# Five of a turn's 25 key units summed over the head dimension by ScalarE, in a hybrid decoder step

## The chip, the cores and the metric

One Trainium2 chip; the kernel runs on one of its cores. The metric is the device time in microseconds (us) of one execution. TensorE (PE) does matrix products, VectorE (DVE) elementwise work and sums, ScalarE (ACT) activations and copies, GpSimd (POOL) here only starts transfers, SyncE (SP) starts transfers too. Each engine works through its own stream in order, and waits on semaphores for the others.

## The reference

The reference is one inference step of a two-layer hybrid decoder, for a prompt of 1024 tokens and for 8 sample sequences of one token each with 8192 past positions. The part around the change is the attention of the samples to their past keys, which lie in pages of 128 positions. Cut to it:

```python
def score(qb, kb):
    return jnp.einsum('bthd,bshd->bhts', qb, kb, preferred_element_type=jnp.float32) * scale + bias_h

def sb_weights(z, q_pos, k_pos):
    causal = k_pos[None, :] < q_pos[:, None]
    u = jnp.where(causal, jax.nn.log_sigmoid(-z), 0.0)
    after = lax.cumsum(u, axis=z.ndim - 1, reverse=True) - u
    return jnp.where(causal, jnp.exp(jax.nn.log_sigmoid(z) + after), 0.0)
```

With one query, a score is the sum over the 64 values of a head of query times key. There are 8 heads, 64 pages for each of the 8 samples, so 512 pages of 128 x 512 float32 (256 KB each), and as many pages of values. Beside it the same layer runs a recurrence (RWKV-7) over the prompt, in chunks of 64 tokens.

## The kernel before, in words

The kernel is a row of phases, each with a stream for every engine. The pages are a side job that is spread over several of them by the class `Pages`. A unit is two pages of keys; there are 256 units, 32 for each sample. For a unit `keys_dve` (L1097) waits for its two pages, multiplies them by the query on VectorE into `pg_prod` (L1106, 128x1024), and sums the 64 values of each head, also on VectorE, into `pg_z` (L1109). The units are dealt out by hand: 16 in `v_phase`, 42 in `pb_phase`, 24 in `attention_phase`, and from unit 82 on 25 in each turn of the recurrent stage, `rwkv_phase`.

Keys come over SyncE: `load_keys` (L1011) goes through the pages in order, waits until the slot of the ring (`RING` = 8 pages, so four units) is free, reads the page's number and starts the transfer. The slot counts as free when `k_used` says that the product of the unit four before is done. Values come over GpSimd (`load_values`, L1063) into a ring of 12 pages and are used by TensorE (`values_pe`, L1036).

When all units of a sample are done, `bias_dve` (L1118) adds the bias, `logs_act` (L1071) takes Abs, Exp and Ln on ScalarE, `softplus_dve` (L1126), `sums_pe` (L1031) and `exponents_dve` (L1131) make the exponents, and `weights_act` (L1079) the weights.

`rwkv_phase` runs turns `i` = 0 to 8. In a turn the local part of chunk pair `i` (products in a block, five levels of a triangular inverse), the walk of the state through pair `i-1` (two halves) and the preparation of pair `i+1` are interleaved in an order written out by hand for each engine. On VectorE the calls `more(n)` put the key units in between: with offsets in the turn, 0 to 2 after `softplus_dve`; 3, 4 after `blocks_t`; `state(i-1, 0)`, `blocks` and `exponents_dve`; 5; `mask_keys`, `gate_ones(i+1)`; 6, 7; `level(i, 1)`, `tanh(i+1)`, `keys(i+1)`; 8, 9; `lora_bias(i+1)`, `state(i-1, 1)`; 10; `level(i, 2)`, `sigmoid_ones(i+1)`; 11, 12; `log_decays(i+1)`, `center(i-1)`; 13, 14; `level(i, 3)`; 15, 16; `modified_keys(i+1)`, `normed(i-1)`, `level(i, 4)`; 17, 18; `products(i+1)`, `level(i, 5)`, `bonus(i+1)`, `outputs(i-1)`; 19 to 24; `bias_dve(i+1)`. Turn 7 has no units; the update of the samples' recurrent state takes their place. On ScalarE the order of a turn is `eyes`, `token_major`, `copy_read(i-1, 0)`, `copy_values(i-1, 0)`, `copy_blocks`, `copy_outputs(i-1, 0)`, `gate_exps(i+1)`, `copy_y(i, 1)`, `weights_act`, `copy_read(i-1, 1)`, `fold_act`, `copy_values(i-1, 1)`, `gate_sigmoids(i+1)`, `key_squares(i+1)`, `copy_y(i, 2)`, `sigmoid_exps(i+1)`, `copy_outputs(i-1, 1)`, `sigmoids(i+1)`, `copy_y(i, 3)`, `pick_act`, `key_norms(i+1)`, `decays(i+1)`, `output_squares(i-1)`, `copy_y(i, 4)`, `output_norms(i-1)`, `affine(i-1)`, `copy_y(i, 5)`, `logs_act(i+1)`.

Of the kernel before, what the change touches and what calls it, by code (L numbers as in the profile page):

```python
# [789 lines left out]
def v_phase(T):  # L790
# [8 lines left out]
    with ExitStack() as ctx:  # L799
# [47 lines left out]

        @block.vector
        def _(dve):
            pages.start_dve(dve)  # L850
            for k in range(KT):
                dve.wait_ge(w_rounded, k + 1)
                rest_weights(dve, wl[:, k, :], w[:, k, :], wh[:, k, :], w_split)
            pages.keys_dve(dve, KEYS_V)
# [101 lines left out]
class Pages:  # L956
# [8 lines left out]
    def __init__(self, T, ctx):  # L965
        nc = T.nc
        self.T, self.nc = T, nc
        self.sems = sems = Sems(nc, "pages")
        self.k_in = [sems(f"k_in{n}") for n in range(self.RING)]
        self.v_in = [sems(f"v_in{n}") for n in range(self.VRING)]  # L970
        (self.qc_in, self.q_turned, self.q_copied, self.q_stored, self.q_in, self.table_in, self.k_used, self.v_used,
         self.reduced, self.biased, self.logged, self.softplus_ready, self.summed, self.z_ready, self.w_ready,
         self.cleared, self.folded, self.selected, self.picked, self.step, self.act_step) = (
            sems(n) for n in ("qc_in", "q_turned", "q_copied", "q_stored", "q_in", "table_in", "k_used", "v_used",
                              "reduced", "biased", "logged", "softplus_ready", "summed", "z_ready", "w_ready",
                              "fold_cleared", "folded", "selected", "picked", "page_step", "page_act_step"))
        sb = lambda n, s, d=F32: ctx.enter_context(nc.sbuf_tensor("pg" + n, s, d))
        self.kp = sb("_k", [P, self.RING, D_A])
        self.qc, self.q = sb("_qc", [P, 4, NS]), sb("_q", [P, 2, D_A])
        self.fold = sb("_fold", [P, D_A])  # L980
        self.qr = self.fold[0:NS, :]
        self.prod = sb("_prod", [P, 2, D_A])
        self.z = sb("_z", [P, self.ZRING, H_A, NPG])
        self.zb, self.sp = sb("_zb", [P, H_A * NPG]), sb("_sp", [P, H_A * NPG])
        self.wts = sb("_w", [P, 2, H_A * NPG])
        self.table = sb("_table", [1, NS * NPG], I32)
        self.q_rows = nc.dram_tensor("scratch_pg_q", [NS, D_A], F32, kind="Internal").ap()
        self.fetched, self.unit = 0, 0
# [16 lines left out]

    def load_q(self, sp, b):
        if b >= 2:
            sp.wait_ge(self.k_used, self.RING + NPG * (b - 1))
        sp.dma_start(self.q[:, b % 2, :], self.q_rows[b:b + 1, :].to_broadcast([P, D_A])).then_inc(self.q_in, 16)

    def load_keys(self, sp, units):  # L1011

        for g in range(self.fetched, min(2 * units + self.RING, NS * NPG)):
            if g % NPG == NPG // 2 and 2 <= g // NPG + 1 < NS:
                self.load_q(sp, g // NPG + 1)
            n = g % self.RING
            sp.wait_ge(self.k_used, g + 1)
            page = sp.value_load(self.table[0:1, g:g + 1], min_val=0, max_val=self.T.n_phys - 1)
            sp.dma_start(self.kp[:, n, :], self.T.io["k_pages"][bass.ds(page, 1), :, :].rearrange("a p n -> (a p) n"))\
              .then_inc(self.k_in[n], 16)  # L1020
            self.fetched = g + 1
# [75 lines left out]
    def keys_dve(self, dve, n):  # L1097

        for u in range(self.unit, min(self.unit + n, NS * self.UNITS)):
            b, g, at = u // self.UNITS, 2 * u % NPG, 2 * u % self.RING  # L1100
            if g == 0:
                dve.wait_ge(self.q_in, 16 * b + 16)
            for e in range(2):
                dve.wait_ge(self.k_in[at + e], 16 * (2 * u // self.RING) + 16)
            dve.wait_ge(self.reduced, u + 1)
            dve.tensor_tensor(self.prod[:, :, :], self.kp[:, at:at + 2, :],  # L1106
                              self.q[:, b % 2, :].unsqueeze(1).to_broadcast([P, 2, D_A]), ALU.mult).then_inc(self.k_used, 2)
            dve.wait_ge(self.k_used, self.RING + 2 * u + 2)
            dve.tensor_reduce(self.z[:, b % self.ZRING, :, g:g + 2].rearrange("p h n -> p n h"),  # L1109
                              self.prod[:, :, :].rearrange("p n (h d) -> p n h d", h=H_A), AX.X, ALU.add)\  # L1110
               .then_inc(self.reduced, 1)
            self.unit = u + 1

    def start_dve(self, dve):
        dve.sem_inc(self.k_used, self.RING)
        dve.sem_inc(self.reduced, 1)

    def bias_dve(self, dve, b):  # L1118
        assert self.unit >= self.UNITS * (b + 1)
        dve.wait_ge(self.reduced, self.UNITS * (b + 1) + 1)  # L1120
# [18 lines left out]


KEYS_V, KEYS_PB, KEYS_ATT, KEYS_TURN = 16, 42, 24, 25


def attention_phase(T):
# [239 lines left out]
def rwkv_phase(T):  # L1384
# [23 lines left out]
    with ExitStack() as ctx:  # L1408
# [48 lines left out]
        @block.sync  # L1457
        def _(sp):
            pages.load_keys(sp, NS * Pages.UNITS)
            sp.wait_ge(pages.k_used, Pages.RING + NS * NPG)  # L1460
# [338 lines left out]
        def _(act):  # L1799
# [157 lines left out]
            for i in range(NPAIR + 1):  # L1957
# [7 lines left out]
                    sample_rows(0)  # L1965
                if walk:
                    copy_values(i - 1, 0)
                if local:
                    copy_blocks(i)
                if walk:  # L1970
                    copy_outputs(i - 1, 0)
                both(i, gate_exps)
                if local:
                    copy_y(i, 1)
                    pages.weights_act(act, i)
                else:
# [9 lines left out]
                    copy_values(i - 1, 1)  # L1986
                both(i, gate_sigmoids)
                both(i, key_squares)
                if local:
                    copy_y(i, 2)  # L1990
                else:
                    output_norms(SMP)
                both(i, sigmoid_exps) if walk else sigmoid_exps(1)
                if walk:
                    copy_outputs(i - 1, 1)
                both(i, sigmoids) if walk else sigmoids(1)
                if local:
                    copy_y(i, 3)
                else:
                    affine(SMP)  # L2000
                if walk:
# [3 lines left out]
                if walk:  # L2005
                    output_squares(i - 1)
                else:
                    sigmoid_exps(SMP)
                    sigmoids(SMP)
                if local:  # L2010
                    copy_y(i, 4)
                if walk:
# [9 lines left out]
                    sample_rows(2)  # L2022
                if i == 1:
                    sample_columns()
                if i + 1 < NS:
                    pages.logs_act(act, i + 1)

# [1172 lines left out]
```

## Time and profile before

| | before |
|---|---|
| median of 3 runs | 4680.5 us (4674.18 to 4684.39) |
| the profiled execution's own time | 4680.36 us |
| its span | 4678.8 us |
| busy: PE, DVE, ACT, POOL | 3892.4, 2356.6, 1174.4, 399.8 us |
| share of the span | 83%, 50%, 25%, 9% |
| DMA moved | 512.41 MB, mean 110 GB/s |

```profile
PE   6887885776777869999896999789898087999899
DVE  2488888888887224443312444444443524434411
ACT  3223662222222222222202222322221012222300
DMA  2465316988887321111222222210100231111122
```

The four lines are the span in 40 slices of 117 us; a digit is the busy share of the slice in tenths, for DMA the mean of the 16 DMA engines. Slices 7 to 13 hold the recurrent stage with the keys. Busy shares over the whole span mix stages that have different limits; the rows further down are of the recurrent stage.

### The profile page before, as it was taken

How to read it: one execution, taken by the hardware profiler on the slowest of the kernel's cores; microseconds unless marked ns; L12 is line 12 of the kernel's file. 1: busy time of each engine (PE TensorE's matmuls, PEld its weight loads, DVE VectorE, ACT ScalarE, POOL GpSimd, SP SyncE). 2: the span in 40 equal slices, each digit the busy share in tenths (PEclk: the TensorE clock that was granted, in tenths of full speed). 3: DMA queues.
4: the chain of work that ended last, by engine and by line, in shares of the span. 5: the costliest groups of instructions: out<-in, count | busy, mean ns of one | idle time of the engine just before them, and what ended most of it. 6: DMA issues, size and time to landing. Idle time of an engine off the chain costs nothing. (4 is left out here: it accounts for less than half of the span.)

```text
span 4678.8 us, 77496 instructions
## 1 busy us (share of the span) xinstructions
PE 3892.4 (83%) x29645; PEld 3336.8 (71%) x29645; DVE 2356.6 (50%) x3054; ACT 1174.4 (25%) x1872; POOL 399.8 (9%) x739
## 2 busy tenths in 40 slices
PE   6887885776777869999896999789898087999899
PEld 5786333444444659999896889677777087999899
DVE  2488888888887224443312444444443524434411
ACT  3223662222222222222202222322221012222300
POOL 0011102333333100000000000000000000000000
PEclk8998997888888789999998999877777598999999
DMA  2465316988887321111222222210100231111122
GB/s 93 153 208 165 112 48 214 311 290 294 288 289 245 113 100 46 46 45 45 65 81 92 74 83 83 81 33 19 37 19 15 78 138 50 45 45 46 44 82 64
DMA packets 212105, 512.41 MB, mean 110 GB/s; under 512 B 34153, under 2 KB 67321, under 8 KB 205298
## 3 DMA queue, kind: packets, MB, share of 16 engines
q1 hardware_dynamic: 148306, 305.03, 19.9%
q0 software_dynamic: 62640, 203.84, 12.5%
q8 instruction: 151, 2.47, 0.2%
q14 instruction: 96, 0.79, 0.1%
q10 hardware_dynamic: 912, 0.28, 0.0%
HBM read 454.87 MB, written 54.56 MB: 109 GB/s over the span
## 5 line engine op out<-in xcount | busy, mean ns | idle before, releaser
L263 PE MATMUL ps<-ffn_hh,up_wh 128*128 128x344 f32 x2112 | 678.6, 321 | 59.8 <-DVE up_wl L255 59.8
L265 PE MATMUL ps<-ffn_hl,up_wh 128*128 128x344 f32 x2112 | 677.0, 321 | 0.0
L264 PE MATMUL ps<-ffn_hh,up_wl 128*128 128x344 f32 x2112 | 676.3, 320 | 0.0
L263 PEld LDWEIGHTS ps<-ffn_hh,up_wh 128*128 128x128 f32 x2112 | 398.8, 189 | 60.9 <-issue 60.9
L265 PEld LDWEIGHTS ps<-ffn_hl,up_wh 128*128 128x128 f32 x2112 | 398.8, 189 | 0.0
L264 PEld LDWEIGHTS ps<-ffn_hh,up_wl 128*128 128x128 f32 x2112 | 398.7, 189 | 0.0
L458 PE MATMUL ps<-down_ah,down_wh 128*128 128x344 f32 x1056 | 342.5, 324 | 31.3 <-DVE down_al L492 18.7
L459 PE MATMUL ps<-down_ah,down_wl 128*128 128x344 f32 x1056 | 339.5, 321 | 0.0
L460 PE MATMUL ps<-down_al,down_wh 128*128 128x344 f32 x1056 | 339.4, 321 | 0.0
L1106 DVE TENSOR_TENSOR pg_prod<-pg_k,pg_q 128x1024 f32<-128x1024 f32 x256 | 313.4, 1224 | 34.6 <-DVE rw_mxt L2141 4.6
L1068 POOL DMA_DIRECT2D pg_v<-in_v_pages x512 | 275.3, 538 | 557.1 <-issue 487.1
L1109 DVE TENSOR_REDUCE pg_z<-pg_prod 128x16 f32<-128x1024 f32 x256 | 313.0, 1223 | 8.8
L263 PE MATMUL ps<-hh,odd_wh 128*128 128x344 f32 x792 | 261.0, 330 | 64.7 <-DVE odd_wl L255 64.7
L264 PE MATMUL ps<-hh,odd_wl 128*128 128x344 f32 x792 | 257.4, 325 | 0.0
L265 PE MATMUL ps<-hl,odd_wh 128*128 128x344 f32 x792 | 257.1, 325 | 0.0
L458 PEld LDWEIGHTS ps<-down_ah,down_wh 128*128 128x128 f32 x1056 | 200.2, 190 | 35.9 <-issue 29.9
L1046 PE MATMUL ps<-pg_v,pg_w 128*8 128x512 f32 x1024 | 208.3, 659 | 18.8 <-DMA pg_v<-in_v_pages 18.2
L263 PEld LDWEIGHTS ps<-hh,odd_wh 128*128 128x128 f32 x792 | 152.6, 193 | 73.3 <-ACT odd_row L2360 41.2
L459 PEld LDWEIGHTS ps<-down_ah,down_wl 128*128 128x128 f32 x1056 | 201.0, 190 | 0.0
L460 PEld LDWEIGHTS ps<-down_al,down_wh 128*128 128x128 f32 x1056 | 200.3, 190 | 0.0
L255 DVE TENSOR_TENSOR down_wl<-down_w,down_wh 128x896 fp32r<-128x896 f32 (+1 forms) x48 | 54.4, 1136 | 280.9 <-ACT down_wh L250 280.9
L663 DVE TENSOR_TENSOR ffn_a<-up_cv,ps 128x344 f32 (+1 forms) x132 | 67.4, 511 | 245.4 <-PE ps L265 245.4
(457 smaller groups left out, 7300.6 us busy)
## 6 DMA issues: line engine op xcount, KB each, us to landing
pg_k<-in_k_pages SPq DMA_DIRECT2D x512, 256.0 KB, 4.5
pg_v<-in_v_pages POOLq DMA_DIRECT2D x512, 256.0 KB, 4.6
up_w<-in_w_ff SPq DMA_DIRECT2D x44, 1034.0 KB, 4.8
odd_w<-in_w_odd SPq DMA_DIRECT2D x33, 526.0 KB, 4.0
scratch_odd_rows<-odd_cv POOLq DMA_DIRECT2D x32, 516.0 KB, 4.4
down_w<-in_w_down SPq DMA_DIRECT2D x32, 448.0 KB, 3.3
dn_x<-scratch_odd_rows SPq DMA_DIRECT2D x8, 1536.0 KB, 7.8
scratch_x<-out_x POOLq DMA_DIRECT2D x16, 516.0 KB, 2.9
```

Source lines behind the costliest of these rows:

```text
L255: dve.tensor_tensor(lo, w, hi.bitcast(F32), ALU.subtract).then_inc(rest_ready, 1)
L263: pe.matmul(out, wh, xh, start=(k == 0), stop=False)
L264: pe.matmul(out, wl, xh, start=False, stop=False)
L265: mm = pe.matmul(out, wh, xl, start=False, stop=(k == n - 1))
L458: pe.matmul(out, hi, ah[:, k, g[c]], start=(k == 0), stop=False)
L459: pe.matmul(out, lo, ah[:, k, g[c]], start=False, stop=False)
L460: mm = pe.matmul(out, hi, al[k][:, g[c]], start=False, stop=(k == FT - 1))
L663: dve.tensor_tensor(a[:, bass.ds(2 * i + j, 1), col].rearrange("p a t -> p (a t)"), cv[:, j, col], ps[:, 3 + c, 0:GC], ALU.mult).then_inc( ...
L1046: pe.matmul(self.T.ps[c:c + H_A, 7, :], wts[:, :, g], self.vp[:, at % self.VRING, :], start=(g < 4), stop=(g >= NPG - 4), tile_position=(0 ...
L1068: pool.dma_start(self.vp[:, at % self.VRING, :], self.T.io["v_pages"][bass.ds(page, 1), :, :] .rearrange("a p n -> (a p) n")).then_inc(sel ...
L1106: dve.tensor_tensor(self.prod[:, :, :], self.kp[:, at:at + 2, :], self.q[:, b % 2, :].unsqueeze(1).to_broadcast([P, 2, D_A]), ALU.mult).th ...
L1109: dve.tensor_reduce(self.z[:, b % self.ZRING, :, g:g + 2].rearrange("p h n -> p n h"), self.prod[:, :, :].rearrange("p n (h d) -> p n h d" ...
```

## The change

In the recurrent stage the units at offsets 1, 4, 8, 12 and 17 of each of the seven turns with keys are handled otherwise (`for_act`, 35 units). VectorE multiplies their pages in place, in the ring (`pg_k`), and does not sum them. ScalarE's new `keys_act` takes one page a call: for each of the 8 heads a Copy of 128x64 onto itself with `accum_out` into `pg_z`. Ten calls stand in ScalarE's turn. The slot of such a unit is free when ScalarE has done both pages (`unit_free`), and `bias_dve` waits for ScalarE's sums too. The counter `k_used`, which started at 8 and rose by 2, becomes `multiplied`, which starts at 0 and rises by 1 a unit; `reduced` loses its start value, and `reduced_act` is new.

```diff
+        self.for_act = [u for u in range(FIRST_TURN, FIRST_TURN + (NS - 1) * KEYS_TURN)
+                        if (u - FIRST_TURN) % KEYS_TURN in ACT_UNITS]
+    def sums_before(self, u):
+        return sum(v < u for v in self.for_act)
...
+    def unit_free(self, sp, u):
+        before = u - self.RING // 2
+        if before in self.for_act:
+            sp.wait_ge(self.reduced_act, 2 * self.sums_before(before) + 2)
+        elif before >= 0:
+            sp.wait_ge(self.multiplied, before + 1)
...
-            sp.wait_ge(self.k_used, g + 1)
+            self.unit_free(sp, g // 2)
...
-            dve.wait_ge(self.reduced, u + 1)
-            dve.tensor_tensor(self.prod[:, :, :], self.kp[:, at:at + 2, :],
-                              self.q[:, b % 2, :].unsqueeze(1).to_broadcast([P, 2, D_A]), ALU.mult).then_inc(self.k_used, 2)
-            dve.wait_ge(self.k_used, self.RING + 2 * u + 2)
-            dve.tensor_reduce(self.z[:, b % self.ZRING, :, g:g + 2].rearrange("p h n -> p n h"),
-                              self.prod[:, :, :].rearrange("p n (h d) -> p n h d", h=H_A), AX.X, ALU.add)\
-               .then_inc(self.reduced, 1)
+            query = self.q[:, b % 2, :].unsqueeze(1).to_broadcast([P, 2, D_A])
+            if u in self.for_act:
+                keys = self.kp[:, at:at + 2, :]
+                dve.tensor_tensor(keys, keys, query, ALU.mult).then_inc(self.multiplied, 1)
+            else:
+                dve.wait_ge(self.reduced, u - self.sums_before(u))
+                dve.tensor_tensor(self.prod[:, :, :], self.kp[:, at:at + 2, :], query, ALU.mult).then_inc(self.multiplied, 1)
+                dve.wait_ge(self.multiplied, u + 1)
+                dve.tensor_reduce(self.z[:, b % self.ZRING, :, g:g + 2].rearrange("p h n -> p n h"),
+                                  self.prod[:, :, :].rearrange("p n (h d) -> p n h d", h=H_A), AX.X, ALU.add)\
+                   .then_inc(self.reduced, 1)
...
+    def keys_act(self, act, n):
+        for m in range(self.unit_act, min(self.unit_act + n, 2 * len(self.for_act))):
+            u, e = self.for_act[m // 2], m % 2
+            b, g, at = u // self.UNITS, (2 * u + e) % NPG, (2 * u + e) % self.RING
+            act.wait_ge(self.multiplied, u + 1)
+            for hd in range(H_A):
+                keys = self.kp[:, at, hd * DH:(hd + 1) * DH]
+                last = act.activation(keys, keys, ACT.Copy, accum_out=self.z[:, b % self.ZRING, hd, g:g + 1])
+            last.then_inc(self.reduced_act, 1)
+            self.unit_act = m + 1
...
+        done = self.sums_before(self.UNITS * (b + 1))
+        dve.wait_ge(self.reduced, self.UNITS * (b + 1) - done)
+        if done:
+            dve.wait_ge(self.reduced_act, 2 * done)
...
+FIRST_TURN, ACT_UNITS = KEYS_V + KEYS_PB + KEYS_ATT, (1, 4, 8, 12, 17)
```

The places of the ten pages in ScalarE's turn:

```diff
                     copy_values(i - 1, 0)
+                pages.keys_act(act, 1)
                 if local:
                     copy_blocks(i)
                 if walk:
                     copy_outputs(i - 1, 0)
+                pages.keys_act(act, 1)
...
                     pages.weights_act(act, i)
+                    pages.keys_act(act, 1)
...
                 both(i, key_squares)
+                pages.keys_act(act, 1)
                 if local:
                     copy_y(i, 2)
+                    pages.keys_act(act, 1)
...
                 both(i, sigmoids) if walk else sigmoids(1)
+                pages.keys_act(act, 1)
                 if local:
                     copy_y(i, 3)
+                    pages.keys_act(act, 1)
...
                     sigmoids(SMP)
+                pages.keys_act(act, 1)
                 if local:
                     copy_y(i, 4)
...
                     sample_columns()
+                pages.keys_act(act, 2)
                 if i + 1 < NS:
                     pages.logs_act(act, i + 1)
```

## Rows read from the trace of the kernel before

**Rows 1.** The page's groups: line, engine, operation, shapes, count, busy us, mean ns.
```profile
L1106 DVE TENSOR_TENSOR pg_prod<-pg_k,pg_q 128x1024 f32<-128x1024 f32 x256 | 313.4, 1224 | 34.6 <-DVE rw_mxt L2141 4.6
...
L1109 DVE TENSOR_REDUCE pg_z<-pg_prod 128x16 f32<-128x1024 f32 x256 | 313.0, 1223 | 8.8
```

**Rows 2.** L1128; one turn's busy us: PE, PEld, DVE, ACT, POOL, clock, DMA.
```profile
L1128 DVE SCALAR_TENSOR_TENSOR pg_sp<-pg_zb,pg_sp x8: 691/693/693, 716.6 to 1452.1; 128x512 f32<-128x512 f32 x8
...
1137.43:1243.10 105.67, 74.84 (x952) 43.28 (x952) 92.67 (x101) 25.56 (x49) 35.51 (x65) 0.86 0.86 292
```

**Rows 3.** VectorE's waits, 800 to 1440 us: waited for, us, times, longest.
```profile
DVE rw_dh L2031 <- PE ps L1646: 19.5, 6, 3.6
```

**Rows 4.** VectorE in order of time, one turn: start us, us, line, operation, [idle before].
```profile
1147.35 1.22 DVE L1106 TENSOR_TENSOR pg_prod<-pg_k,pg_q 128x1024 f32<-128x1024 f32 x1 [0.41 <-DVE rw_mrb L2031]
...
1149.97 1.23 DVE L1106 TENSOR_TENSOR pg_prod<-pg_k,pg_q 128x1024 f32<-128x1024 f32 x1
...
1152.36 0.86 DVE L2031 TENSOR_TENSOR rw_dh<-rw_Hx,ps 64x256 f32<-64x256 f32 x2
...
1158.38 1.22 DVE L1106 TENSOR_TENSOR pg_prod<-pg_k,pg_q 128x1024 f32<-128x1024 f32 x1
...
1170.21 1.23 DVE L1106 TENSOR_TENSOR pg_prod<-pg_k,pg_q 128x1024 f32<-128x1024 f32 x1 [0.33 <-DVE rw_kk L2031]
...
1179.92 0.87 DVE L2031 TENSOR_TENSOR rw_dh<-rw_Hx,ps 64x256 f32<-64x256 f32 x2 [3.46 <-PE ps L1646]
...
1186.30 0.69 DVE L2061 TENSOR_SCALAR rw_e<-rw_e 128x1024 f32<-128x1024 f32 x1
...
1189.53 1.23 DVE L1106 TENSOR_TENSOR pg_prod<-pg_k,pg_q 128x1024 f32<-128x1024 f32 x1
...
1191.93 1.22 DVE L2068 TENSOR_TENSOR_SCAN rw_D<-consts,rw_e 128x512 f32<-128x512 f32 x1
...
1204.60 1.23 DVE L1106 TENSOR_TENSOR pg_prod<-pg_k,pg_q 128x1024 f32<-128x1024 f32 x1
...
1243.10 0.69 DVE L1128 SCALAR_TENSOR_TENSOR pg_sp<-pg_zb,pg_sp 128x512 f32<-128x512 f32 x1 [2.02 <-ACT pg_sp L1077]
```

**Rows 5.** ScalarE in order of time, the same turn.
```profile
1154.22 0.38 ACT L1898 ACTIVATE rw_on<-ps 128x256 f32<-128x256 f32 x1 [6.50 <-DVEq L2154]
...
1169.98 0.63 ACT L1828 ACTIVATE rw_ksq<-rw_kk 128x512 f32<-128x512 f32 x1 [3.17 <-DVEq L2050]
...
1188.16 1.06 ACT L1840 ACTIVATE rw_e<-rw_e 128x1024 f32<-128x1024 f32 x1
...
1189.60 0.34 ACT L1093 ACTIVATE h<-ps 64x4 f32<-64x4 f32 x2
...
1190.68 0.63 ACT L1847 ACTIVATE rw_ksq<-rw_ksq 128x512 f32<-128x512 f32 x1
1193.96 0.63 ACT L1852 ACTIVATE rw_eL<-rw_D 128x512 f32<-128x512 f32 x1 [2.65 <-DVEq L2073]
...
1195.02 0.61 ACT L1855 ACTIVATE rw_D<-rw_D 128x512 f32<-128x512 f32 x1
1195.54 0.61 ACT L1904 ACTIVATE rw_on<-rw_on 128x512 f32<-128x512 f32 x1
```

**Rows 6.** SyncE's issues at 1149 us; landing times, key pages: all, then around 1172 us.
```profile
1149.31 1.43 SPq L1019 DMA_DIRECT2D pg_k<-in_k_pages  x2
...
DMA to landing us min/median/max: 2.4/4.5/9.7
...
DMA to landing us min/median/max: 2.6/2.7/2.8
```

**Rows 7.** ScalarE's groups by shape, 700 to 1560 us: the small ones.
```profile
L1833 ACT ACTIVATE rw_se<-rw_se 128x64 f32<-128x64 f32 x1 | 0.2, 239 | 0.0
...
L1823 ACT ACTIVATE rw_ssg<-rw_seg 128x8 f32<-128x8 f32 x1 | 0.2, 192 | 0.0
```

**Rows 8.** TensorE in order of time: the end of the outputs' products.
```profile
1151.19 0.28 PE L1646 MATMUL ps<-rw_mrb,rw_ur 64*64 64x64 f32 x3
```

More of the change, by code:

```diff
@@ L849, in _ @@
         def _(dve):
-            pages.start_dve(dve)
             for k in range(KT):
@@ L970, in __init__ @@
         self.v_in = [sems(f"v_in{n}") for n in range(self.VRING)]
-        (self.qc_in, self.q_turned, self.q_copied, self.q_stored, self.q_in, self.table_in, self.k_used, self.v_used,
-         self.reduced, self.biased, self.logged, self.softplus_ready, self.summed, self.z_ready, self.w_ready,
+        (self.qc_in, self.q_turned, self.q_copied, self.q_stored, self.q_in, self.table_in, self.multiplied, self.v_used,
+         self.reduced, self.reduced_act, self.biased, self.logged, self.softplus_ready, self.summed, self.z_ready, self.w_ready,
          self.cleared, self.folded, self.selected, self.picked, self.step, self.act_step) = (
-            sems(n) for n in ("qc_in", "q_turned", "q_copied", "q_stored", "q_in", "table_in", "k_used", "v_used",
-                              "reduced", "biased", "logged", "softplus_ready", "summed", "z_ready", "w_ready",
+            sems(n) for n in ("qc_in", "q_turned", "q_copied", "q_stored", "q_in", "table_in", "multiplied", "v_used",
+                              "reduced", "reduced_act", "biased", "logged", "softplus_ready", "summed", "z_ready", "w_ready",
                               "fold_cleared", "folded", "selected", "picked", "page_step", "page_act_step"))
@@ L987, in __init__ @@
         self.q_rows = nc.dram_tensor("scratch_pg_q", [NS, D_A], F32, kind="Internal").ap()
-        self.fetched, self.unit = 0, 0
+        self.fetched, self.unit, self.unit_act = 0, 0, 0
+        self.for_act = [u for u in range(FIRST_TURN, FIRST_TURN + (NS - 1) * KEYS_TURN)
+                        if (u - FIRST_TURN) % KEYS_TURN in ACT_UNITS]
+    def sums_before(self, u):
+        return sum(v < u for v in self.for_act)
     def open_values(self, ctx):
@@ L1007, in load_q @@
         if b >= 2:
-            sp.wait_ge(self.k_used, self.RING + NPG * (b - 1))
+            sp.wait_ge(self.multiplied, self.UNITS * (b - 1))
         sp.dma_start(self.q[:, b % 2, :], self.q_rows[b:b + 1, :].to_broadcast([P, D_A])).then_inc(self.q_in, 16)
+    def unit_free(self, sp, u):
[4 more added lines that the diff above has]
+            sp.wait_ge(self.multiplied, before + 1)
     def load_keys(self, sp, units):
@@ L1112, in keys_dve @@
-            self.unit = u + 1
-    def start_dve(self, dve):
-        dve.sem_inc(self.k_used, self.RING)
-        dve.sem_inc(self.reduced, 1)
+            query = self.q[:, b % 2, :].unsqueeze(1).to_broadcast([P, 2, D_A])
[9 more added lines that the diff above has]
+                   .then_inc(self.reduced, 1)
@@ L1118, in bias_dve @@
     def bias_dve(self, dve, b):
         assert self.unit >= self.UNITS * (b + 1)
-        dve.wait_ge(self.reduced, self.UNITS * (b + 1) + 1)
+        done = self.sums_before(self.UNITS * (b + 1))
+        dve.wait_ge(self.reduced, self.UNITS * (b + 1) - done)
+        if done:
+            dve.wait_ge(self.reduced_act, 2 * done)
         if b:
@@ L1459, in _ @@
             pages.load_keys(sp, NS * Pages.UNITS)
-            sp.wait_ge(pages.k_used, Pages.RING + NS * NPG)
+            for u in range(NS * Pages.UNITS, NS * Pages.UNITS + Pages.RING // 2):
+                pages.unit_free(sp, u)
             sp.dma_start(st8, io["wkv_in"].rearrange("p (k v) -> p k v", k=64)).then_inc(S["state_in"], 16)
```

## The prediction, made before the change was run

> **What bounds the kernel now.** I started from the page's costliest groups: 256 key products and 256 sums over the head dimension on VectorE, 1.22 us each [rows 1]. The recurrent stage was then cut by its `softplus_dve` (L1128), one per turn: seven turns with keys lie between 716.6 and 1452.1 us, and the turn from 1137.43 to 1243.10 us, which I use as the pattern, lasts 105.67 us with VectorE busy for 92.67, ScalarE for 25.56 and the DMA engines for 0.86 of it [rows 2]. The reader should see one nearly full engine, one three-quarters empty, and a DMA that is not far from full. The list of waits shows what holds VectorE from 800 to 1440 us: six waits of about 3.3 us for TensorE before `state(i-1, 1)`; a wait for a key page is not in it [rows 3]. In the list of instructions in order of time a unit of keys repeats every 2.62 us (1147.35 to 1149.97), and only two gaps are large, 3.46 us at 1179.92 and 2.02 us at 1243.10 [rows 4]. So VectorE's own order sets the turn. That makes its work worth moving, but only if nothing is then late for it. What comes nearest is read from ScalarE's and SyncE's own order of time [rows 5, 6].
>
> **What is removed.** Units 1, 4, 8, 12 and 17 of a turn (u1, u4, ...) lose their TENSOR_REDUCE and the two small waits around it. A unit goes from 2.62 us to about 1.32, so 5 x 1.3 = 6.5 us of VectorE per turn [rows 4].
>
> **What is added on ScalarE.** A turn gets 10 calls of `keys_act` (K1 to K10), each one page: 8 Copies of 128x64 with an accumulated output. No row of before shows that form. Nearest: a 128x64 Exp takes 0.239 us and the least ACTIVATE (128x8) 0.192 [rows 7]; successors start about 0.09 us before the end of the one before (1195.02 to 1195.54 for 0.61 long) [rows 5]. From below, if accumulating costs nothing, a head is 0.24 - 0.09 = 0.15 us and a page 1.2. From above, if each head is two instructions without overlap, 0.24 + 0.19 = 0.43 us and a page 3.45. It cannot be below nothing, as the Copies are extra. I take 0.29 us a head, between the two, since a second, short instruction may overlap: A = 2.3 us a page, 23 us a turn. That is well inside ScalarE's 80 us of idle time; the total is not the trouble, the moments are.
>
> The Trainium skill ("ScalarE: Activation LUTs", What ACT_TABLE_LOAD costs) gives an ACTIVATE with immediate operands 186 ns + 0.833 ns an element and an overlap of 93 ns, thus an estimate of 0.15 us a head and 1.2 us a page, with no word on the accumulated output; the trace agrees on the 0.24 us of the plain form [rows 7]. By it the sum below would be the 4721 us of its low end, not 4769.
>
> **What is moved: the release of the key slots.** The ring holds 8 pages, four units, so unit u+4 is loaded into the slots of unit u. Before, these were free when the product of u was done; now, for the five, only when ScalarE has summed both pages. SyncE's queue is in order: behind that wait stand the loads of all later units. From a release to the landing: the product from 1147.35 ends 1148.57 and the first load issues at 1149.31, 0.74 later; the second 1.10 later (1.43 less its own 0.33); landing takes 2.4 to 9.7 us over the kernel, median 4.5, and 2.7 at 1172 us where keys are scarce [rows 4, 6]. I take 3.5 us, nearer the small end, because SyncE will then have been silent for several us. A release thus costs R = 0.74 + 1.10 + 3.5 = 5.34 us before the second page is there. Per turn, by the rows of [rows 4, 5]:
> - u5 needs u1. K2 stands behind `copy_outputs(i-1, 0)`, which waits for the state update and ends at 1154.60 (1154.22 + 0.38). From there it is A + R = 7.6 us; VectorE wants u5 at 1158.38, 3.8 after it. Stall 3.9.
> - u8 needs u4. K4 stands behind `key_squares(i+1)`, which waits for `keys(i+1)`, VectorE's last instruction before u8 (end 0.33 before 1170.21, so 1169.89); the squares end 1170.61. So 0.72 + A + R = 8.4 against 0.32. Stall 8.0. Behind u8 on VectorE stand `lora_bias` and the state update. u9's pages come 2.2 us after u8's, and the product lasts 1.25: 0.9 more.
> - The wait of 3.46 us at 1179.92 falls into that stall, as TensorE goes on: -3.5 [rows 4].
> - u12 needs u8. K6 stands behind the two `sigmoids`, which wait for `sigmoid_ones` (end 1186.99) and end 1189.22. So 2.23 + A + R = 9.9; VectorE has one unit, 2.54 us, to do (u12 at 1189.53). Stall 7.3. K5 waits for u8's product, but the `sigmoid_exps` behind it need `lora_bias`, which is later anyway.
> - u16 needs u12. K7 now waits for u12's product, and behind it stand the pick, `key_norms`, `decays` and `output_squares`: 1.7 us for the first two (1189.60 to 1191.31), 1.7 for the decays (1193.96 to 1195.63), 0.5 for the squares; with K7, K8 and some 0.2 of waits 8.7, plus R is 14.0, against 12.7 (1191.93 to 1204.60). Stall 1.3.
> - u21 needs u17. K9 and K10 follow the last `copy_y`; bonus, outputs and two whole units cover them. Nothing.
> - Before u5 some of the saving is lost: TensorE ends `change_and_outputs(i-1, 0)` at 1151.47 [rows 8] and VectorE came 0.9 us after it (1152.36). Two saved sums bring it 2.6 us earlier, so some 1.7 is idle, 1.8 with the semaphore's delay.
>
> Edits at nothing: the counters renamed and the primed ones dropped (a semaphore increment or two), `load_q`'s wait (same event), `bias_dve`'s wait for `reduced_act` (units of earlier turns, or, in the last turn with keys, u17, done six units before), and K1 before `copy_blocks`: it delays `mt` by 2 us, which TensorE, busy until 1151.47 with the outputs, hides; without that cover it would be 2 us a turn.
>
> **Sum.** A turn: -6.5 + 1.8 + 3.9 + 8.0 + 0.9 - 3.5 + 7.3 + 1.3 = +13.2 us. Six such turns are 79. The first has no state updates, but the same u8 and u12: I put +10. Total +89 on the profiled execution's 4680.36 us, a span of 4678.8 (1.6 us lie around it); the median of the runs is 4680.5, the same. Forecast 4769 us.
>
> **Bounds.** With A = 1.2 and a landing of 2.6 the stalls are 1.9, 6.0, 5.3 and 0, the turn +5.9, the time 4721. With A = 3.45 they are 5.0, 9.2, 8.5 and 3.6, the turn +19, the time about 4811; with a landing of 5 us besides, about 4850.
>
> **Rivals.**
> (a) Slower, but dear: ScalarE's accumulating Copy costs 0.43 us a head or more: 4811. For it: the only price known is of plain forms. Against: ACTIVATEs overlap.
> (b) Slower, but cheap: Copies at 0.15 us, DMA answering at its least: 4721 to 4740. For it: with VectorE stalled, TensorE consumes no values, so the DMA is emptier than now.
> (c) Faster, the other side: the slot chain is hidden, and ScalarE's page sums come early enough. Then a turn is 6.5 - 1.8 = 4.7 us shorter, seven are 33, and the time 4647. The place is u8 and u12, and it decides where the stalls of a turn sum to less than 8.2 us (6.5 + 3.5 - 1.8): A plus landing would have to fall from 5.8 to some 1.8 us (three stalls, each a constant plus this sum). The least rows give 3.8, so it needs something that I misread in the order of ScalarE's stream or in the ring.
> (d) No change: gains and stalls cancel, or the sums move without moving the end, 4680. It would need the same 1.8 us, by chance exact.
>
> The Trainium skill ("DMA: Bandwidth & Descriptors", Issuing engines are not separate DMA queues) says that DMAs issued from several engines run on the same 16 engines and interleave; the landing times of 2.7 us against a median of 4.5 agree [rows 6], and it is the reason in (b), not a term of the sum.
>
> **Chances.** Forecast with its neighbourhood 0.60, (a) 0.18, (b) 0.14, (c) 0.05, (d) 0.03. A measurement of this kernel can tell about 0.2%, 9 us. Faster 0.05, same 0.04, slower 0.91 (a little of (b) falls into no change). The range takes in the low end of the costs and (a), 4715 to 4830, and leaves out (c), (d) and the very dear case.
>
> **What the profile of after would show.** Right: turns of about 119 us; VectorE waiting before the key product for DMA of the keys, three times a turn, with some 4, 9 and 7 us, at u5, u8 with u9, and u12; the 3.3 us wait for TensorE gone; ScalarE near 48 us busy a turn, its ten groups beginning right behind `copy_outputs`, `key_squares` and `sigmoids`; SyncE waiting for ScalarE, not for VectorE; other stages unchanged. Wrong: no waits for key DMA, which is (c); a head at 0.15 or 0.43 us tells (b) from (a). The prediction fails too if landings at those moments take 5 us and more, or if VectorE's later slack in the turn gives back what it lost.

## The result

| | before | after |
|---|---|---|
| median of the runs | 4682.1 us (4674.2 to 4684.4, 4 runs) | 4822.3 us (4814.3 to 4828.1, 4 runs) |
| profiled execution's span | 4678.8 us | 4821.6 us |
| ratio to before | | 1.0301, 95% interval 1.0282 to 1.0321 |
| the seven turns with keys | 735.5 us | 873.5 us |

The kernel became 140 us slower, and the seven turns hold 138 of them. The prediction said 4769 us, 4715 to 4830, slower with 0.91: the sign and the mechanism held, but the loss is 140 us where 89 were forecast.

The first fence is from the profile's page of the kernel after: slices of the span, then the groups of key products and sums on VectorE (they answer [rows 1]).

```profile
DVE  2487886666666523344421345444444433444511
ACT  3224662333333122222310222222222012222300
DMA  2564316777777722111122222211010132111122
...
L1125 DVE TENSOR_TENSOR pg_prod<-pg_k,pg_q 128x1024 f32<-128x1024 f32 x221 | 270.5, 1224 | 100.4 <-DMA pg_k<-in_k_pages 79.3
...
L1127 DVE TENSOR_REDUCE pg_z<-pg_prod 128x16 f32<-128x1024 f32 x221 | 270.2, 1223 | 7.6
```

VectorE's slices in the stage fell from 8 to 6: it does less and takes longer. DMA fell from 8 to 7. The idle time before the product is now ended mostly by the transfer of the keys, which ended none of it before the change.

The turns are cut by `softplus_dve` again; its group in the kernel after:

```profile
L1157 DVE SCALAR_TENSOR_TENSOR pg_sp<-pg_zb,pg_sp x8: 691/692/693, 716.2 to 1589.7; 128x512 f32<-128x512 f32 x8
```

The fifth turn's window (start to end, length, then busy us of PE, PEld, DVE, ACT, POOL, clock, DMA share, GB/s) answers [rows 2].

```profile
1219.55:1343.63 124.08, 86.25 (x952) 48.22 (x952) 86.30 (x95) 44.76 (x209) 34.44 (x64) 0.79 0.71 244
```

105.7 us became 124.1, with 86.3 us of VectorE's work and not 92.7. The waits of VectorE from 720 to 1560 us (engine, line, waited for, us in total, times, longest) and those of SyncE:

```profile
DVE pg_k L1122 <- DMA pg_k<-in_k_pages: 113.7, 17, 9.8
DVE pg_prod L1125 <- DMA pg_k<-in_k_pages: 79.3, 32, 9.2
DVE rw_on L2199 <- PE ps L1689: 16.0, 6, 2.7
...
SPq L1032 <- ACT pg_k L1140: 430.0, 34, 28.2
```

193 us of VectorE's time go in waiting for key pages, and SyncE, which sends for them, waits 430 us for ScalarE, up to 28.2 us at once. The wait for TensorE before the state update [rows 3] is all but gone (2.6 us in two places are left), as it falls inside the new ones. TensorE's granted clock in this turn was 0.79 and not 0.86; no run separates what the lower clock adds to the loss.

VectorE in order of time in the same turn; the places answer [rows 4].

```profile
1226.73 1.23 DVE L1125 TENSOR_TENSOR pg_prod<-pg_k,pg_q 128x1024 f32<-128x1024 f32 x1 [2.97 <-DMA pg_k<-in_k_pages]
...
1244.83 1.23 DVE L1125 TENSOR_TENSOR pg_prod<-pg_k,pg_q 128x1024 f32<-128x1024 f32 x1 [4.44 <-DMA pg_k<-in_k_pages]
...
1255.95 0.68 DVE L2071 TENSOR_TENSOR rw_kk<-rw_xs,vecs_sb 128x512 f32<-128x512 f32 x1
1264.17 1.26 DVE L1122 TENSOR_TENSOR pg_k<-pg_k,pg_q 128x1024 f32<-128x1024 f32 x1 [7.55 <-DMA pg_k<-in_k_pages]
1268.26 1.22 DVE L1125 TENSOR_TENSOR pg_prod<-pg_k,pg_q 128x1024 f32<-128x1024 f32 x1 [2.83 <-DMA pg_k<-in_k_pages]
...
1289.96 1.23 DVE L1122 TENSOR_TENSOR pg_k<-pg_k,pg_q 128x1024 f32<-128x1024 f32 x1 [8.70 <-DMA pg_k<-in_k_pages]
...
1295.70 0.69 DVE L2199 SCALAR_TENSOR_TENSOR rw_on<-ps,rw_on 128x512 f32<-128x512 f32 x1 [2.66 <-PE ps L1689]
...
1338.54 1.23 DVE L1125 TENSOR_TENSOR pg_prod<-pg_k,pg_q 128x1024 f32<-128x1024 f32 x1 [0.79 <-DMA pg_k<-in_k_pages]
```

From the top: u2, u5, u8 right behind `keys(i+1)`, u9, u12, `center(i-1)` and u24. ScalarE in order of time, around the fourth page sum, answers [rows 5]:

```profile
1256.72 0.63 ACT L1859 ACTIVATE rw_ksq<-rw_kk 128x512 f32<-128x512 f32 x1 [1.23 <-DVEq L2090]
1257.25 0.24 ACT L1140 ACTIVATE pg_k<-pg_k 128x64 f32<-128x64 f32 x1
1257.40 0.18 ACT L1140 ACTIVATION_READ_ACCUMULATOR pg_k<-pg_k 128x1 f32 x1
1257.49 0.24 ACT L1140 ACTIVATE pg_k<-pg_k 128x64 f32<-128x64 f32 x1
...
1259.07 0.18 ACT L1140 ACTIVATION_READ_ACCUMULATOR pg_k<-pg_k 128x1 f32 x1
```

Here is the chain that the prediction named (K1 to K10 are the ten page sums of a turn): `keys(i+1)` ends at 1256.63, the squares of `key_squares` run, then K4, which ends at 1259.25, then the loads of u8's two pages, and u8's product starts at 1264.17.

### The profile page after: what moved, and what is told of

Read it like the earlier page. It is cut to its first block and busy times, and to the rows that moved or that the text cites. A ratio compares the mean times of both kernels' runs of the same rounds, so it can differ in the third digit from the quotient of the medians.

```text
span 4821.6 us, 78332 instructions
## 1 busy us (share of the span) xinstructions
PE 3966.9 (82%) x29645; PEld 3365.3 (70%) x29645; DVE 2311.7 (48%) x3019; ACT 1309.0 (27%) x2992; POOL 400.6 (8%) x739
## 5 line engine op out<-in xcount | busy, mean ns | idle before, releaser
L1125 DVE TENSOR_TENSOR pg_prod<-pg_k,pg_q 128x1024 f32<-128x1024 f32 x221 | 270.5, 1224 | 100.4 <-DMA pg_k<-in_k_pages 79.3
L1060 PE MATMUL ps<-pg_v,pg_w 128*8 128x512 f32 x1024 | 252.5, 696 | 29.3 <-DMA pg_v<-in_v_pages 28.0
L1127 DVE TENSOR_REDUCE pg_z<-pg_prod 128x16 f32<-128x1024 f32 x221 | 270.2, 1223 | 7.6
```

Source lines behind the costliest of these rows:

```text
L1060: pe.matmul(self.T.ps[c:c + H_A, 7, :], wts[:, :, g], self.vp[:, at % self.VRING, :], start=(g < 4), stop=(g >= NPG - 4), tile_position=(0 ...
```

## The experiments

The theory: what costs the time is the late release of the five units' slots, which hangs on what stands ahead of the second page sum in ScalarE's order. Rivals: ScalarE's added work delays the copies that TensorE needs; or products in place, or ScalarE's traffic, slow something down. Each kernel was timed beside the one before the change (4679 to 4682 us). The rows come from more than one chip, so a difference between two of them is good to a few us.

| run | time | ratio to before, 95% interval |
|---|---|---|
| changed kernel | 4822 us | 1.0301 (1.0282 to 1.0321) |
| early order | 4665 us | 0.9965 (0.9951 to 0.9979) |
| release only | 4742 us | 1.0137 (1.0119 to 1.0155) |
| short ScalarE | 4736 us | 1.0129 (1.0108 to 1.0150) |
| pick first | 4795 us | 1.0248 (1.0231 to 1.0265) |
| values' ring 8 | 4850 us | 1.0355 (1.0333 to 1.0377) |
| keys' ring 12, values' 8 | 4717 us | 1.0081 (1.0062 to 1.0100) |
| own buffer, values' ring 8 | 4718 us | 1.0083 (1.0063 to 1.0104) |
| early order, rings of 10 | 4667 us | 0.9978 (0.9966 to 0.9990) |
| before, values' ring 8 | 4704 us | 1.0046 (1.0032 to 1.0060) |
| first turn | 4807 us | 1.0262 (1.0245 to 1.0279) |
| early order, four units | 4664 us | 0.9964 (0.9950 to 0.9978) |
| own buffer and early order, values' ring 8 | 4718 us | 1.0076 (1.0064 to 1.0088) |

**Early order.** The same page sums, at other places of ScalarE's turn.

```diff
-                pages.keys_act(act, 1)
                 if local:
                     copy_blocks(i)
+                pages.keys_act(act, 2)
                 if walk:
                     copy_outputs(i - 1, 0)
-                pages.keys_act(act, 1)
...
                     pages.weights_act(act, i)
-                    pages.keys_act(act, 1)
+                    pages.keys_act(act, 2)
...
                 both(i, key_squares)
-                pages.keys_act(act, 1)
+                pages.keys_act(act, 2)
                 if local:
                     copy_y(i, 2)
-                    pages.keys_act(act, 1)
...
                 both(i, sigmoids) if walk else sigmoids(1)
-                pages.keys_act(act, 1)
                 if local:
                     copy_y(i, 3)
-                    pages.keys_act(act, 1)
...
                     pages.pick_act(act, i - 1)
+                pages.keys_act(act, 2)
...
                     sigmoids(SMP)
-                pages.keys_act(act, 1)
...
                     copy_y(i, 5)
+                pages.keys_act(act, 2)
                 if not walk:
...
                     sample_columns()
-                pages.keys_act(act, 2)
```

> The changed kernel, with the same ten page sums on ScalarE at other places: K1 and K2 between copy_blocks and copy_outputs, K3 and K4 both behind weights_act, K5 and K6 ahead of copy_y(i, 2), K7 and K8 behind the pick, K9 and K10 behind copy_y(i, 5) but ahead of the sample rows. The theory (late release of the slots, set by what stands ahead of the second page sum) expects the waits for key pages at u5, u8, u9, u12 to go, and the turn to fall below before's 105.7 us: about 101.5, so 4650 us. A rival that puts the loss on ScalarE's 20 us of added work a turn, or on its traffic, expects about 4820 still.

4664.6 us: 158 us less than the changed kernel with the same instructions in it, and 0.35% less than before. The window of the seven turns before the change, then in this run:

```profile
716.63:1452.14 735.51, 515.96 (x6474) 300.36 (x6472) 642.41 (x699) 174.12 (x332) 242.04 (x443) 0.85 0.85 289
717.80:1445.10 727.30, 537.66 (x6474) 308.34 (x6472) 597.64 (x665) 308.20 (x1452) 240.90 (x441) 0.84 0.85 291
```

And VectorE's longest waits there:

```profile
DVE pg_prod L1125 <- DMA pg_k<-in_k_pages: 29.6, 21, 3.0
DVE rw_dh L2067 <- PE ps L1677: 28.3, 9, 4.8
```

ScalarE is busy for 308.2 us as in the changed kernel (308.95), and the waits for keys fell from 193 to 31 us (29.6, and 1.5 in a smaller row). As the cause of the 140 us, ScalarE's work, its traffic and the products in place fall: all are still there, and only the places changed. But the turns became only 8 us shorter than before's 735.5, not some 30 as expected. Part of what is missing is time in which TensorE waits for ScalarE's `output_squares`, which K7 and K8 now precede (first line before the change, second line here; six turns have this wait):

```profile
PE ps L1663 <- ACT rw_on L1904: 12.1, 6, 2.0
PE ps L1694 <- ACT rw_on L1935: 22.5, 6, 3.9
```

**Release only.** VectorE does all the arithmetic as before the change; at the ten places ScalarE only waits for the product and raises the counter that frees the slots.

```diff
-            if u in self.for_act:
-                keys = self.kp[:, at:at + 2, :]
-                dve.tensor_tensor(keys, keys, query, ALU.mult).then_inc(self.multiplied, 1)
-            else:
-                dve.wait_ge(self.reduced, u - self.sums_before(u))
+            if True:
+                dve.wait_ge(self.reduced, u)
...
-            for hd in range(H_A):
-                keys = self.kp[:, at, hd * DH:(hd + 1) * DH]
-                last = act.activation(keys, keys, ACT.Copy, accum_out=self.z[:, b % self.ZRING, hd, g:g + 1])
-            last.then_inc(self.reduced_act, 1)
+            act.sem_inc(self.reduced_act, 1)
...
-        dve.wait_ge(self.reduced, self.UNITS * (b + 1) - done)
-        if done:
-            dve.wait_ge(self.reduced_act, 2 * done)
+        dve.wait_ge(self.reduced, self.UNITS * (b + 1))
```

> All 256 units are multiplied and summed on VectorE as before; ScalarE does no page sum, but at the ten places of the changed kernel it waits for the product and then only increments the counter that frees the slots. The release theory expects most of the loss without any moved work: stalls as in the changed kernel less 1.9 us for each page sum, 2.5 at u5, 5.6 and 1.5 at u8 and u9, 6.8 at u12, less the 3.5 us wait for TensorE: about 13 us a turn, 4773 us. The rival of ScalarE's work or of products in place expects before's 4682.

4742.5 us, where the theory gave 4773 and the rival 4682: a loss of some 62 us without any moved work, two thirds of the expected one. VectorE's largest wait from 716 to 1600 us:

```profile
DVE pg_prod L1122 <- DMA pg_k<-in_k_pages: 87.0, 27, 5.8
```

87 us of waits, none longer than 5.8. I had expected 16 us a turn for keys, 115 in all; it was 12. So the places of the releases alone make the kernel slower, but by less than I had worked out. Probably this is because VectorE, with its sums back, has 1.3 us more to do in each of the five units while the loads are under way, which the expectation left out; no run tests it.

**Short ScalarE.** The changed kernel with one tiny Copy a page; the sums of the 35 units are left out.

```diff
-            for hd in range(H_A):
-                keys = self.kp[:, at, hd * DH:(hd + 1) * DH]
-                last = act.activation(keys, keys, ACT.Copy, accum_out=self.z[:, b % self.ZRING, hd, g:g + 1])
+            last = act.activation(self.z[:, b % self.ZRING, :, g], self.kp[:, at, 0:H_A], ACT.Copy)
```

> The changed kernel, but for each page ScalarE does one Copy of 128x8 in the place of 8 accumulating Copies: the sums over the head dimension of the 35 units are left out. So a page costs some 0.2 us and not 1.93. The release theory expects only the A part of the stalls to go: about 1.7 us at u5, u8, u12 and before center, 3.5 at the end of the turn; 10 to 12 us a turn, 4745 us, still slower than before. A rival in which ScalarE's 20 us a turn are the loss expects about 4640.

4736.3 us, as the theory expected (4745) and not as the rival did (4640). Nearly all of ScalarE's added work is gone, and 57 us of the loss stay. 86 went, 12.3 us a turn, for 10 pages that take 1.7 us less each: what a shorter page sum gives back fits the stalls in which one stands (10 to 12 us by the expectation), though this run by itself can't tell it from 17 us less load on ScalarE a turn. The early order can, as it has the whole load and not the loss.

**Pick first.** `pick_act` was behind K7, which waits for u12's product.

```diff
                     copy_y(i, 3)
-                    pages.keys_act(act, 1)
...
                     pages.pick_act(act, i - 1)
+                if local:
+                    pages.keys_act(act, 1)
```

> The changed kernel with pick_act ahead of the seventh page sum. That sum waits for u12's product, and TensorE's mean(i-1) waits for the pick, so VectorE's center(i-1) waited 2.7 us for TensorE in the changed kernel. If this chain is real, those 2.7 us go in six turns: 16 us, 4806 us. If center waits for TensorE's own work, 4822 stays.

4795.5 us, 27 less, where 16 were expected; the wait of `center` for TensorE (16.0 us in six places) is no longer in the list of waits. So the chain u12, K7, pick, mean, center is real. The waits for keys fell too, from 193 to 176 us, and that of the state update for TensorE rose from 2.6 to 12.9; why these moved I did not test.

**The ring of the values, a control.** The next two kernels need room in the on-chip memory, which this kernel fills (twelve key pages beside twelve value pages do not fit); four value pages give it (`VRING` 8 for 12). This one changes nothing else.

```diff
-    VRING = 12
+    VRING = 8
```

> A control for the next two: the changed kernel with a ring of 8 pages for the values, not 12, which makes room for more key pages or product buffers. TensorE waits for values are hidden behind VectorE's stalls, so about 4822 us; every us above it is the price of the smaller ring.

4850.1 us: the smaller ring costs 28 us, where I had expected about nothing.

**Ring of twelve key pages.** The control with more key pages.

```diff
-    RING = 8
+    RING = 12
```

> The control with a ring of 12 pages for the keys, so that unit u+6 is loaded into the slots of unit u and each release has two more units of VectorE's work (some 7 us) as its cover. The release theory expects the waits at u8 and u12 (7.6 and 8.7 us) to go but for a rest, the turn to fall to 102 to 104 us: 4660 us plus what the control costs. If ScalarE's added work or the products in place cost the time, it stays at the control's.

4716.6 us, 133 less than its control, but 29 more than expected (4660 plus the control's 28). VectorE's largest wait for keys from 716 to 1620 us (us in total, times, longest):

```profile
DVE pg_prod L1125 <- DMA pg_k<-in_k_pages: 7.1, 3, 4.1
```

Same ScalarE order, same products in place, and 177 us of waits for keys became 7: more cover for the release is enough. With the early order, this excludes the products in place as a cause of the 140 us.

**Own buffer.** The control, with the five units' products in a buffer two units deep.

```diff
-        if before in self.for_act:
-            sp.wait_ge(self.reduced_act, 2 * self.sums_before(before) + 2)
-        elif before >= 0:
+        if before >= 0:
             sp.wait_ge(self.multiplied, before + 1)
...
-                keys = self.kp[:, at:at + 2, :]
-                dve.tensor_tensor(keys, keys, query, ALU.mult).then_inc(self.multiplied, 1)
+                k = self.sums_before(u)
+                if k >= 2:
+                    dve.wait_ge(self.reduced_act, 2 * k - 2)
+                dve.tensor_tensor(self.prod_act[:, 2 * (k % 2):2 * (k % 2) + 2, :], self.kp[:, at:at + 2, :], query,
+                                  ALU.mult).then_inc(self.multiplied, 1)
...
-                keys = self.kp[:, at, hd * DH:(hd + 1) * DH]
+                keys = self.prod_act[:, 2 * (m // 2 % 2) + e, hd * DH:(hd + 1) * DH]
```

> The control, but VectorE writes the products of the five units into a buffer of their own (two units deep), so the slot is free at the product, as before the change; ScalarE does all its page sums from there, at the places of the changed kernel. Release theory: all long waits for key pages go, turn about 101.5 us, 4650 us plus what the control costs. A rival in which ScalarE's sums delay its own stream, and so TensorE, expects at least half of the loss to stay: 4750.

4718.2 us, 132 less than the control: two different ways to uncouple the slots from ScalarE's sums agree within 2 us. It is again more than expected (4650 plus 28), by 40 us. Its window of the seven turns:

```profile
715.30:1490.70 775.40, 585.21 (x6474) 312.06 (x6472) 596.74 (x665) 305.81 (x1452) 243.49 (x443) 0.86 0.83 274
```

And VectorE's longest waits in it:

```profile
DVE rw_mxt L2183 <- PE ps L1618: 45.1, 12, 7.5
DVE rw_dh L2073 <- PE ps L1679: 43.9, 12, 5.7
```

No wait for keys is among them; VectorE now waits for TensorE.

**The kernel before with eight value pages.** Is that rest the change's or the ring's? The edit is the control's, made to the kernel before.

```diff
-    VRING = 12
+    VRING = 8
```

> A second control: the kernel before the change with a ring of 8 pages for the values. With the changed kernel the smaller ring cost 28 us (4850 against 4822). If it costs TensorE the same or more where VectorE does not stall, 4710 us or more here, and then the two kernels with the slots freed early (4717, 4718) stand level with or below their own before, and what they leave is the ring of the values, not the change. If it costs nothing here, 4682, they are 36 us slower through ScalarE's share of the work.

4704.1 us, 24 above before. Its window of the seven turns, from an execution 10 us below that median:

```profile
721.83:1467.04 745.21, 583.00 (x6474) 307.97 (x6472) 642.13 (x699) 173.73 (x332) 242.78 (x443) 0.88 0.85 286
```

So against the kernel before with the same ring the two uncoupled kernels are still some 14 us slower (12.5 and 14.1 by the medians, 16 and 17 by the ratios, whose intervals just do not meet). VectorE has 45 us less to do than there (642.1 to 596.7 in the windows of the turns) and gives more than that back in waits for TensorE (37 us there, 108 and 119 in the two).

Part of the ring's price is seen on ScalarE. `gate_exps` of the next pair needs the prompt's rows, which GpSimd starts from the same stream as the value pages; with eight value pages ScalarE waits for them in six turns (first line before the change, second line here):

```profile
ACT rw_eg L1809 <- DMA rw_xs<-scratch_xs_rows: 1.4, 1, 1.4
ACT rw_eg L1809 <- DMA rw_xs<-scratch_xs_rows: 41.0, 6, 7.4
```

Behind that wait stand `copy_y(i, 1)`, K3 and the copies for TensorE.

**Early order with rings of ten.** The early order with one more unit of keys and two pages of values less.

```diff
-    RING = 8
+    RING = 10
...
-    VRING = 12
+    VRING = 10
```

> The early order (page sums placed as in the second order experiment: pairs behind copy_blocks, weights_act, key_squares, the pick and the last copy_y) with rings of 10 pages for keys and values. It had 29.6 us of waits for key pages left, in 21 places of up to 3 us, which I put on landings of 5 us and more at the end of a turn. One unit more of cover should take most of them: 4640 to 4650 us, against 4665 with 8 and 12.

4667.3 us, level with the early order: the expected gain (4640 to 4650) did not come. The window of the turns:

```profile
716.20:1436.70 720.50, 553.13 (x6473) 307.53 (x6472) 596.74 (x665) 306.85 (x1452) 242.59 (x442) 0.87 0.86 293
```

And VectorE's waits in it:

```profile
DVE rw_dh L2067 <- PE ps L1677: 43.2, 12, 5.7
DVE rw_mxt L2177 <- PE ps L1616: 15.7, 8, 5.5
...
DVE pg_prod L1125 <- DMA pg_k<-in_k_pages: 2.4, 5, 1.1
```

The keys' waits fell from 31 to about 2 us, as expected, and the two largest waits for TensorE rose from 36 to 59. What TensorE waits for more than before the change are, above all, the pages of values; its weight loads' wait for them in the seven turns (us, times) is, in the kernel before:

```profile
  DMA pg_v<-in_v_pages: 55.1, 56
```

in the early order:

```profile
  DMA pg_v<-in_v_pages: 83.4, 77
```

and in this run:

```profile
  DMA pg_v<-in_v_pages: 104.8, 93
```

**First turn.** K9 and K10 ahead of the sample rows.

```diff
+                pages.keys_act(act, 2)
                 if not walk:
                     sample_rows(1)
                     sample_rows(2)
                 if i == 1:
                     sample_columns()
-                pages.keys_act(act, 2)
```

> The changed kernel with K9 and K10 ahead of the sample rows, which matters in the first turn (and by a column load in the second). There u17's slot was freed only after both sample rows, and VectorE waited 9.3 us for u21's keys and 2.2 us more until the turn's end. If that is the cause, the first turn falls from 129 to about 118 us and the time by 11 us to 4811; if not, 4822 stays.

4806.6 us, 16 less, 11 expected. The first turn went from 129.0 us (716.18 to 845.17) to 120.2 us (724.16 to 844.39). VectorE at u21 of the first turn, in the changed kernel (first line) and here; the two lie at the same time only because the turn began 8 us later here:

```profile
830.48 1.23 DVE L1125 TENSOR_TENSOR pg_prod<-pg_k,pg_q 128x1024 f32<-128x1024 f32 x1 [9.25 <-DMA pg_k<-in_k_pages]
```

```profile
830.52 1.23 DVE L1125 TENSOR_TENSOR pg_prod<-pg_k,pg_q 128x1024 f32<-128x1024 f32 x1 [1.88 <-DMA pg_k<-in_k_pages]
```

**Early order, four units.** u17 stays with VectorE.

```diff
-FIRST_TURN, ACT_UNITS = KEYS_V + KEYS_PB + KEYS_ATT, (1, 4, 8, 12, 17)
+FIRST_TURN, ACT_UNITS = KEYS_V + KEYS_PB + KEYS_ATT, (1, 4, 8, 12)
...
                     copy_y(i, 5)
-                pages.keys_act(act, 2)
```

> The early order with four units and not five: u17 stays on VectorE, so K9 and K10 are gone. The early order still had waits for keys at u2 and u5 of the next turn (2.7 and 1.7 us), which I put on u17's late release. Without it they go, 1.5 us of VectorE's work comes back: a turn 2 to 3 us shorter or level, 4650 to 4665 us. If the TensorE chain sets the turn by then, it stays at 4665.

4663.6 us, level with five units. The turns are 7 us shorter in the profile (720.1 to 727.3), but the profiled execution of five units was 7 us above its median, so this is no gain. The waits for keys fell from 31 to 10 us: u17's late release was behind most of them. This or the early order with five is the best kernel of the study, both faster than before by 0.35%, which is small but clear of the intervals.

**Own buffer and early order.** The edits of the two kernels of those names together, with `VRING = 8`; the places of the page sums are the one thing in which it differs from the own buffer.

> Own product buffers for the five units, eight value pages, and the page sums at the early places. With own buffers the slots are free at the product wherever the sums stand, so the places can act only through ScalarE's own order. With the sums at the places of the changed kernel this took 4718 us, 14 above the kernel before with eight value pages (4704). If that rest is ScalarE's order (copies for TensorE behind page sums, the pick behind K7), 4690 to 4700 us here; if it is the split of the work or the buffer itself, 4718 stays.

4717.7 us: no gain over the own buffer with the places of the changed kernel. That the 14 us come from those places in particular falls. Nor did the values' pages come later: TensorE's weight loads wait for them 146 us in both, against 153 in the kernel before with the same ring. What the traces do show are waits of TensorE for ScalarE, which move with the order but do not go. In the own buffer it is the pick that is late:

```profile
PE ps L1691 <- ACT h L1106: 14.1, 6, 2.9
PE ps L1657 <- ACT rw_ur L1919: 4.0, 5, 1.0
```

and here it is `copy_read(i-1, 1)`, behind K3 and K4, and `output_squares`, behind K7 and K8:

```profile
PE ps L1657 <- ACT rw_ur L1919: 14.0, 6, 2.9
PE ps L1696 <- ACT rw_on L1937: 8.2, 6, 2.0
```

In the kernel before with eight value pages the first two waits are not in the list, and the one for `output_squares` is 0.6 us. So 18 and 22 us of such waits are new, near the 14 us in size. That ScalarE's page sums cost them in either order is thus likely, but not shown: no run takes these waits away.

## Why the prediction was right, and where its size was off

**The mechanism held, and the size was low.** The six turns after the first are 19.0 us longer on average, where the sum had 13.2, and the first is 24.1 longer, where it had 10: these two make up the 49 us that are missing. u5, u8 and u12 stand in the waits as predicted, with ScalarE's `copy_outputs`, `key_squares` and `sigmoids` ahead of the page sum. By turns (the pattern turn of each):

| term | predicted | measured |
|---|---|---|
| five sums less | -6.5 | -7.3 (a unit without its sum takes 1.15 us, from u17's product at 1313.72 to the next at 1314.87, and not 2.62: 1.47 each) |
| idle before u5 | +1.8 | 0 (VectorE had waited at u2) |
| u5 | +3.9 | +4.4 |
| u8 | +8.0 | +7.6 |
| u9 | +0.9 | +2.8 |
| wait for TensorE gone | -3.5 | -3.5 |
| u12 | +7.3 | +8.7 |
| u16 | +1.3 | 0 |
| center, not predicted | | +2.7 |
| u2, u7, u24, not predicted | | +4.2 (3.0, 0.4, 0.8) |
| sum | +13.2 | +19.6; the turn is 18.4 longer |

**The price of a page.** I took 2.3 us; it is 1.93 (eight heads at 0.24, see below), so this term of the sum was too dear, and rival (a), a dear Copy, is out, though its 4811 us lie nearest to the measured time. Nor was it (b): a head was not 0.15 us, and the landing was not short everywhere.

**The landing time.** Working back from K4's end, 4.9 us less 1.84 for the issues (0.74 and 1.10) gives about 3.1 us at u8. At u12 K6 ended at 1282.95 and the product began 7.0 us later, which leaves about 5.2 us. So the 3.5 us taken for all were 1.7 too few at u12. They rested on SyncE having been silent, but GpSimd's transfers ran on: it had started four value pages from 1277.08 to 1280.54 and started four more from 1284.03 on, and the DMA engines moved 221 GB/s between K6's end and the product, against 164 between K4's end and u8's product, a stretch in which no value page had been started for 13.6 us until 1261.45. That the value pages make the difference fits these rows; no run tests it. The pages of u9, asked for behind u8's, took longer as well (4.9 to 5.3 us for the loads issued from 1262 to 1264.5), hence 2.8 us and not 0.9. The median over these turns was 5.1 us before the change already; the 4.5 that the prediction started from was that of the whole kernel.

**Luck in the range.** The upper end, 4830, was put there for a page at 3.45 us. No page cost that; the measured 4822 comes near it through terms that the sum lacked, so that it lies within the range is in part luck.

**A dependency that I did not follow.** K7 waits for u12's product, and behind K7 I priced `key_norms` and `decays` but took the pick only as 0.3 us of time. TensorE's `mean` waits for it, and VectorE's `center` for that. "Pick first" showed it, and was worth 27 us, of which 16 are this wait.

**"u21: nothing."** That step was wrong twice. In the first turn `sample_rows` stand ahead of K9 and K10, and u21 waited 9.3 us; "first turn" took 7.4 of them away. In the pattern turn u21 itself came in time, but SyncE, which needs 1.1 us an issue, started late on the pages behind it, and short waits followed at u24 (0.8 us) and u2 of the next turn (2.7 us). That u17's release is behind them is shown for the early order, where "four units" took 21 of the 31 us away; in the changed kernel it was not tested.

**The other side.** Rival (c) asked that stalls sum to under 8.2 us a turn. The early order reaches that (31 us in seven turns) and is faster, but by 14 us and not 33. The 1.8 us a turn that I took off for TensorE were too few: VectorE's waits for TensorE in the seven turns rose from 26 to 44 us in the early order and to 66 with rings of ten. That VectorE alone bounded the stage was thus true only for the first few us. The keys and values came at 289 GB/s before the change and at 291 in the early order; whether TensorE's chain or the supply of values sets the turn by then, no run separates.

## What to carry to other kernels

When a consumer moves to another engine, the buffer it reads is freed in that engine's order: look for what stands ahead of the last read, and whether that waits for something that the engine which fills or first reads the buffer does just before it needs it again. Then price the chain (last read, release, issue, landing) against that engine's work in between; the new engine's idle share says nothing about it. Take the landing time from the stage in question, with the other transfers that run there. And before moving work off an engine that is near 90% busy, find the one that comes next: with the better order the 45 us moved were worth 14.

## What the runs showed of the hardware

An activation with an accumulated output is two instructions on ScalarE, the ACTIVATE (242 ns for 128x64; the plain Exp of that shape took 239 [rows 7]) and a read of the accumulator (188 ns), but they overlap: from one head to the next it is 0.24 us (1257.25 to 1257.49). By the overlap of plain activations in [rows 5] that is an estimated 0.09 us more than a plain Copy. These are the two groups in the changed kernel, 720 to 1560 us.

```profile
L1140 ACT ACTIVATE pg_k<-pg_k 128x64 f32<-128x64 f32 x544 | 130.3, 242 | 77.2 <-DVE pg_k L1122 73.7 <-issue 2.1 <-DVE pg_prod L1125 1.3
L1140 ACT ACTIVATION_READ_ACCUMULATOR pg_k<-pg_k 128x1 f32 x544 | 102.1, 188 | 0.0
```
